# A decode-and-prefill step on one core: V sums moved behind the logits, the pooling mixers into free PSUM banks, the token-row turns spread, heads later, 12 w_out tiles among the cache pages

## The reference

```python
h = rmsnorm(x, norm1_g)
q, k, v, u = split(h @ w_in)               # 8 heads of 128; u is 1024 wide
a = attend(q, k, v)                        # prompt: causal with ALiBi; sample: see below
p = pool_mixer(u)                          # windows 2, 4, 8, 16, then a 256x256 product per group
x = x + concat([a, p]) @ w_out             # w_out: 2048 x 2048
h2 = rmsnorm(x, norm2_g)
x = x + (silu(h2 @ w_gate) * (h2 @ w_up)) @ w_down      # 5632 wide
y = rmsnorm(x, norm_f_g)
```

## Time and profile before

| what | value |
|---|---|
| median of 3 runs | 1420.48 us (1417.19 to 1421.45) |
| profiled execution | 1420.67 us, span of the trace 1418.6 us |
| PE busy | 1352.9 us (95%) |
| DVE, ACT, POOL busy | 712.7, 494.0, 105.0 us |
| moved by DMA | 334.13 MB, mean 236 GB/s |
| mean granted TensorE clock | 0.981 of full speed |

### The profile page before, as it was taken

One profiled execution on the slowest core, in us unless ns is written; L12 is line 12 of the kernel. 1 busy time (PEld: TensorE's weight loads), 2 busy tenths in 40 slices (PEclk: granted clock), 3 DMA queues, 4 the chain that ended last, 5 costly groups with the idle time before them and its releaser, 6 DMA issues.

```text
span 1418.6 us, 27166 instructions
## 1 busy us (share of the span) xinstructions
PE 1352.9 (95%) x10651; PEld 1256.1 (89%) x10651; DVE 712.7 (50%) x1102; ACT 494.0 (35%) x653; POOL 105.0 (7%) x172
## 2 busy tenths in 40 slices
PE   7999999998688899999999999999999999999998
PEld 6987777774466689999999999999999999999997
DVE  7633432324333437746455555555564646455556
ACT  6322222213221225633333334343333333333334
POOL 5038200001000003100000000000000000000003
PEclk9999999998899999999999999999999999999999
DMA  9779999997989854544444444444444444444442
GB/s 353 298 302 380 412 413 410 410 382 254 405 330 412 341 211 177 193 164 166 169 168 163 163 164 170 168 163 163 164 167 170 164 163 164 166 171 164 163 163 97
DMA packets 91750, 334.13 MB, mean 236 GB/s; under 512 B 10465, under 2 KB 10466, under 8 KB 91426
## 3 DMA queue, kind: packets, MB, share of 16 engines
q1 hardware_dynamic: 91682, 333.22, 63.0%
HBM read 327.77 MB, written 5.40 MB: 235 GB/s over the span
## 4 chain that ended last, share of the span: by engine, by line
PE 85%; DMA 5%; DVE 4%; SPq 3%; issue 2%; ACT 1%; DVEq 0%; ACTq 0%
PE banks L1338 26%; PE banks L1339 26%; PE banks L1340 25%; PE banks L1402 3%; DMA w_raw<-in_weights 3%; PE banks L1418 3%; DVE w_lo L808 1%; SPq L422 1%; DMA vpage<-in_cache_v 1%; SPq L436 1%; ACT w_hi L553 1%; DMA kpage<-in_cache_v 1%; PE banks L1346 1%; PE banks L1488 0%; SPq L426 0%
## 5 line engine op out<-in xcount | busy, mean ns | idle before, releaser
L808 DVE TENSOR_TENSOR w_lo<-w_raw,w_hi 128x1024 fp32r<-128x1024 f32 x360 | 442.7, 1235 | 542.6 <-ACT w_hi L553 541.9
L1338 PE MATMUL banks<-hh,w_hi 128*128 128x288 f32 x2176 | 651.2, 299 | 25.2 <-DVE w_lo L808 19.2
L1339 PE MATMUL banks<-hl,w_hi 128*128 128x288 f32 x2176 | 648.3, 298 | 0.0
L1340 PE MATMUL banks<-hh,w_lo 128*128 128x288 f32 x2176 | 645.6, 297 | 0.0
L553 ACT ACTIVATE w_hi<-w_raw 128x1024 fp32r<-128x1024 f32 x360 | 379.4, 1058 | 695.6 <-PE banks L1340 459.1
L1338 PEld LDWEIGHTS banks<-hh,w_hi 128*128 128x128 f32 x2176 | 414.2, 190 | 51.0 <-issue 40.0
L1339 PEld LDWEIGHTS banks<-hl,w_hi 128*128 128x128 f32 x2176 | 414.4, 190 | 0.1
L1340 PEld LDWEIGHTS banks<-hh,w_lo 128*128 128x128 f32 x2176 | 413.3, 190 | 0.0
L1340 PE MATMUL banks<-ah,w_lo 128*128 128x288 f32 x704 | 207.8, 295 | 0.0
L1339 PE MATMUL banks<-al,w_hi 128*128 128x288 f32 x704 | 207.4, 295 | 0.0
L1338 PE MATMUL banks<-ah,w_hi 128*128 128x288 f32 x704 | 206.6, 293 | 0.5 <-DVE al L1171 0.5
(11 more groups left out here) (163 smaller groups left out, 523.0 us busy)
## 6 DMA issues: line engine op xcount, KB each, us to landing
w_raw<-in_weights SPq DMA_DIRECT2D x360, 512.0 KB, 3.2
kpage<-in_cache_k SPq DMA_DIRECT2D x128, 512.0 KB, 6.9
vpage<-in_cache_v SPq DMA_DIRECT2D x120, 512.0 KB, 7.1
kpage<-in_cache_v SPq DMA_DIRECT2D x8, 512.0 KB, 7.8
out_y_prompt<-yt SPq DMA_DIRECT2D x4, 512.0 KB, 3.5
xT<-in_x SPq DMA_DIRECT2D x3, 576.0 KB, 8.8
out_k_new<-z SPq DMA_DIRECT2D x1, 1152.0 KB, 6.6
out_v_new<-z SPq DMA_DIRECT2D x1, 1152.0 KB, 8.9
```

The lines of the kernel that those rows point to most:

```text
L808: V.tensor_tensor(w_lo[:, s, :], w_raw[:, s, :], w_hi[:, u, :].bitcast(F32), ALU.subtract).then_inc(lo_ready, 1)
L1338: PE.matmul(o, wh, xh[:, c, :], start=start and i == 0, stop=False)
L1339: PE.matmul(o, wh, xl[:, c, :], start=False, stop=False)
L1340: last = PE.matmul(o, wl, xh[:, c, :], start=False, stop=stop and i == len(chunks) - 1)
```

## The change

- In steps behind a block's first, PE does `logits`, then `values`, then the tiles; before it was `logits`, one tile, `values`, the rest. At a block's first step it does two tiles (in the head blocks one), `joint_max`, the rest, then `p_turned`.
- DVE makes the low part of a block's first tile at the end of the step before, ahead of `take_values`; `head_lo` stands before `joint_max`.
- ACT makes the high parts of a step's tiles first in the step, ahead of the heads' copies.
- The mixers move from steps 12 to 18 to steps 10, 11, 14 and 15, into the spare logits bank and bank 7 (`PB`).
- The six row turns, in a row at the end of block 4 before, stand now at step 21 (two) and steps 22, 23, 26, 27 (one each), all copied out by ACT.
- Head h has its logits at step 21 + h; before at 19 + h, with head 0 at the very end of step 19. The clearing of `qza` moves from DVE to POOL.
- Block 4 has 8 tiles instead of 10, and the two kvu tiles that are left stand in step 20. Out tiles among the pages: 12 instead of 10 (2, 5, 5 in blocks 5, 6, 7 against 1, 3, 6). Four instead of six stand behind step 31. SP loads out tile 12 at step 30, 13 at step 31, 14 ahead of V units 30 and 31, and 15 behind them.

```diff
-TILE_COUNT = (3, 2, 2, 2) * 4 + (3, 2, 2, 3) + (0, 0, 1, 0, 1, 1, 1, 0) + (2, 1, 2, 1)
+TILE_COUNT = (3, 2, 2, 2) * 4 + (2, 2, 2, 2) + (2, 0, 1, 1) + (2, 1, 1, 1) + (2, 1, 1, 1)
-HEAD0 = NQUADS * KVU_STEPS
-MIX_BLOCK = 7
+HEAD0 = NQUADS * KVU_STEPS + 1
+MIX_AT = {10: 0, 11: 1, 14: 2, 15: 3}
+ROWS_AT = {22: 1, 23: 3, 26: 4, 27: 5}
...
@@ PE, steps of blocks 0 to 4
                 for j in range(1, NQUADS):
+                    n = NQUADS * i + j
                     logits(i, j)
-                    here = TILES_AT[NQUADS * i + j]
-                    tile(here[0])
                     if i:
                         values(i - 1, j - 1)
-                    tiles(here[1:])
-                if i == KVU_STEPS - 1:
-                    pe.wait_ge(z_ready, 24)
-                    rows_turned(0)
-                    rows_turned(1)
+                    if n in MIX_AT:
+                        mixer(2 * MIX_AT[n])
+                        mixer(2 * MIX_AT[n] + 1)
+                    tiles(TILES_AT[n])
+                if i:
                     values(i - 1, NQUADS - 1)
-                    rows_turned(2)
-                    rows_turned(3)
-                    rows_turned(4)
-                    rows_turned(5)
...
@@ PE, steps of blocks 5 to 7
                     logits(i, j)
-                    if j == 0:
+                    if j:
+                        values(i - 1, j - 1)
+                    else:
                         block_sums(i - 1)
                         combine(i - 2)
-                    if h < H:
+                    if h == 0:
+                        pe.wait_ge(z_ready, 24)
+                        rows_turned(0)
+                        rows_turned(2)
+                    if 0 <= h < H:
                         head_logits(h)
-                    bank1_free(h)
-                    head_turned(h - 1, HB[1])
+                    if h == 0:
+                        pe.wait_ge(tok_act, 2)
+                        own_logits(0)
+                    if 1 <= h <= H:
+                        bank1_free(h)
+                        head_turned(h - 1, HB[1])
                     if j == 0:
+                        tiles(here[:1])
                         joint_max(i - 1)
...
@@ DVE, blocks 5 to 7
                     add_tiles(TILES_AT[n - 1])
-                    lo_tiles(TILES_AT[n])
+                    if h == 0:
+                        take_block(11)
+                        q_spread()
+                    lo_tiles(TILES_AT[n][1 if j == 0 else 0:])
                     if j == 0:
                         select_blocks(i - 1)
+                        if 1 <= h <= H:
+                            head_lo(h - 1)
                         joint_max(i - 1)
...
                         if j == NQUADS - 1:
+                            if i < NB - 1:
+                                lo_tiles(TILES_AT[n + 1][:1])
                             take_values(i - 1)
...
@@ POOL, ahead of the low parts of the pooling mix
+            pool.wait_ge(w_used, T_KVU + KVU_TILES)
+            G.memset(qza[:, :, :], 0.0).then_inc(qza_clear, 1)
...
@@ SP, behind the page steps
-            load_out_pool(range(OUT_TAIL + 3, OUT_TAIL + 4))
+            load_out_pool(range(OUT_TAIL + 2, OUT_TAIL + 3))
             load_v(NQUADS * NB - 2)
             load_v(NQUADS * NB - 1)
-            load_out_pool(range(OUT_TAIL + 4, KC))
+            load_out_pool(range(OUT_TAIL + 3, KC))
```

More of the change, by code:

```diff
@@ L484, in _ @@
                 if n == NQUADS * NB - 2:
-                    load_out_pool(range(OUT_TAIL, OUT_TAIL + 2))
+                    load_out_pool(range(OUT_TAIL, OUT_TAIL + 1))
                 if i and j == NQUADS - 1:
@@ L959, in q_spread @@
                 dve.wait_ge(w_used, T_KVU + KVU_TILES)
-                own.link(V.memset(qza[:, :, :], 0.0))
+                dve.wait_ge(qza_clear, 1)
                 V.tensor_copy(qza[:, :, :].rearrange("p b (h s) -> p b h s", s=36)[:, :, :, 0:NQ],
@@ L1445, in rows_turned @@
             def rows_turned(n):
-                if n >= 2:
-                    pe.wait_ge((tok_act, tok_dve)[n % 2], n // 2)
+                if n not in (0, 2):
+                    i = min(u for u in ROWS_AT if ROWS_AT[u] == n) // NQUADS
+                    pe.wait_ge(pt_ready, i)
+                    pe.wait_ge(comb_saved, i - 1)
+                    if n in (3, 5):
+                        pe.wait_ge(tok_act, n if n == 3 else 5)
                 chunk, a, b = tok_src(n)
@@ L1531, in _ @@
                 here = TILES_AT[NQUADS * i]
-                tile(here[0])
+                tiles(here[:2])
                 if i:
                     joint_max(i - 1)
-                tile(here[1])
+                tiles(here[2:])
                 if i:
                     p_turned(i - 1)
-                tiles(here[2:])
                 for j in range(1, NQUADS):
+                    n = NQUADS * i + j
                     logits(i, j)
-                    here = TILES_AT[NQUADS * i + j]
-                    tile(here[0])
@@ L1591, in _ @@
                         own_logits(OWN_AT[h])
+                    if n in ROWS_AT:
+                        rows_turned(ROWS_AT[n])
                     if j == 0:
+                        tiles(here[1:])
                         p_turned(i - 1)
-                    tiles(TILES_AT[n])
+                    else:
+                        tiles(here)
                     if j == NQUADS - 1:
                         values(i - 1, j)
-            i = NB - 1
-            for j in range(NQUADS):
-                here = TILES_AT[NQUADS * i + j]
-                logits(i, j)
-                if j == 0:
-                    block_sums(i - 1)
-                    combine(i - 2)
-                    tile(here[0])
-                    joint_max(i - 1)
-                    tiles(here[1:])
-                    p_turned(i - 1)
-                else:
-                    tile(here[0])
-                    values(i - 1, j - 1)
-                    tiles(here[1:])
-            values(i - 1, NQUADS - 1)
             k0 = OUT_TAIL
```

198 lines of the change are left out of this document (87 added, 111 removed).

## The result

| | before | changed |
|---|---|---|
| median | 1420.97 us (4 runs) | 1395.84 us (4 runs, 1393.75 to 1397.16) |
| profiled execution | 1420.67 us, span 1418.6 | 1393.75 us, span 1391.9 |
| mean granted TensorE clock | 0.981 | 0.993 |

The ratio is 0.9827, 95% interval 0.9811 to 0.9843: 25 us faster, where 1398 was forecast.

The account below looks back on a forecast made before the run. Holes in the page transfers from 300 us to the last V unit were taken as the bound: -30.2 (floor) + 4.0 (holes left) + 3.4 (tail) = -22.8 against 1420.67, so 1397.9, given as 1398; range 1390 to 1412 us.

Parts of the forecast that it names:

- The holes that remain: Transfer holes left from 300 us to the last V unit after the change, taken as 4 us.
- Third hole: Transfer gap at 462 to 473 us, V buffer freed late behind a tile; 5.4 us, counted as gone.
- Second hole: Transfer gap at 385 to 399 us, PE waiting 6.14 us for `dm`; to go, up to 1 us a block staying.
- First hole: Transfer gap at 320 to 360 us, K unit waiting for step 20's logits; 14.2 us, gone but for about 1 us.
- Clearing on POOL: Clearing `qza` on POOL instead of DVE: taken as 4 us long, costing PE 0 to 2 us, counted 0.
- The new wait for ACT: PE waiting for ACT's two copies ahead of `head_values`: some 0.9 us in six steps, 5 us.
- PE's balance: PE's work in the head blocks, 147 to 165 us plus 5, against the floor's 168.4 us: fits, barely.
- The tail: Last V sums behind the last exponentials: PE idles 5 to 8 us, two sums run slower, +3.4 us (0 to 8).
- A: Rival: half to two thirds of PE's idle and half-clock excess stays in the head blocks; 1403 to 1412 us, chance 0.24.
- B: Rival: head-block stream is full at a lower rate, say 358 GB/s, so holes are worth 20.9 us; 1408.7 us, chance 0.03.
- C: Rival: holes move, K loads waiting on SP behind V loads and tiles; within 4 us of 1420.7, chance 0.06.
- D: Rival: slower, PE waiting at `head_values` in eight head steps for ACT, held by late tiles; 1429 us, chance 0.09.

Follow-up runs that it names:

- a_turns_block: The changed kernel with all six row turns in step 21, ahead of head 0; 1394.69 us, ratio 0.9824 to the kernel before.
- a_heads_20: The changed kernel with two row turns, head 0 and own logits in step 20, later heads one step sooner, last two kvu tiles in step 19; 1396.07 us.
- b_v_early: The kernel before with only the V sum moved directly behind the logits in steps behind a block's first; 1416.74 us, ratio 0.9981.
- a_v_late: The changed kernel with the V sums back behind the step's first tile, in head steps behind the head's turn; 1403.87 us, ratio 0.9896 to the kernel before.
- b_lo_early: The kernel before with high parts first on ACT and the low part of a block's first tile a step earlier on DVE (blocks 5 to 7); 1414.19 us.
- b_turns_behind: The kernel before with the six row turns, head 0's logits and first own logits behind the logits of step 20; 1421.89 us, ratio 1.0015.
- a_clear_dve: The changed kernel with `qza` cleared on DVE again instead of POOL; 1397.55 us, ratio 0.9839 to the kernel before.
- b_three: b_turns_behind, b_v_early and b_lo_early together on the kernel before; 1411.85 us, ratio 0.9951.
- a_pe_light: The changed kernel without the high-weight by low-activation product in 28 kvu and 12 out tiles, 42 us less PE work; 1397.52 us, ratio 0.9846 to the kernel before.

## Why the prediction was right, and where not

- *Transfers bound it; the end moves as the last V sum does.* Shown: the table's loss and span go together, the span less that sum's start is the same to 3.2 us in fourteen kernels, the light kernel gains nothing, and 700 us on is unchanged. The forecast landing was 471.4 + 4.0 = 475.4; it was 474.4. The last few us are not the stream's alone: in the changed kernel the landing and PE's list behind the exponentials end together, and in a_turns_block and a_heads_20 that list ends 2 to 3.5 us behind the landing.
- *The holes that remain.* 4.0 forecast, 3.3 measured. The size is right and the place is not: they lie at 440 to 460, around the issue of V units 28 and 29, which is the third hole that I counted as gone, and none is left of the first, nor in the blocks' first steps.
- *Third hole.* That the V sum's place makes it is shown by b_v_early, which closed it, and by a_v_late, where it grew from 3.3 to 9 us. In the changed kernel it shrank from 6.1 us (384 and 190 GB/s) to 3.3. The V sum's place is not the only lever: in b_lo_early, which leaves it alone, the stretches from 460 to 480 moved 285 and 380 GB/s, 3.9 us lost.
- *Second hole.* Shown by b_lo_early: the wait for `dm` fell from 6.14 to 1.8 us; in the changed kernel it is 0.2.
- *First hole.* It went, as forecast, but the cause that I gave is not what the runs show. "Only the logits of step 20 were late" is wrong: b_turns_behind made them early, and the hole moved to the logits of step 21. Nor does the change need its single parts: not the spread turns, not the clearing on POOL, not the step (a_turns_block, a_clear_dve and a_heads_20 each undo one of these and have no hole there). In b_turns_behind and b_three the six turns, head 0's logits, the wait for `qza` (3.62 us) and head 0's own turn and values all stand in step 20, ahead of the logits of step 21; in a_heads_20 only two turns and the logits do, `qza` is ready, and the head's turn comes behind the logits of step 21. So it seems to be the sum of what stands between two K frees. The head's own turn and values are not the main part of it: the kernel before has them in step 20 too, and its logits of step 21 follow those of step 20 after 7.1 us, against 19.9 in b_turns_behind, where the moved work takes 10.3 us. Six turns alone, in a step that is not a block's first (a_turns_block), make no hole; two turns, head 0 and the own logits in a block's first step (a_heads_20) make none either. That it takes both together, the wait for `qza` included, is argued from the timelines; no run has all of it in step 20 of the changed kernel, and it stays open. The new distribution of tiles and the mixers' new places were not tried alone either. That this hole's 14.2 us came out as forecast is therefore in part luck.
- *Clearing on POOL*: I took 4 us, it took 2.02 us. DVE's filling waited 1.2 us for it and PE not at all. On DVE again it costs nothing that can be measured (0.9839 against 0.9827, intervals of 0.003).
- *The new wait for ACT*: 0.9 us six times forecast, 0.7 measured (3.6 + 0.7 = 4.3 us in all), off the bound, since these waits stand in a_pe_light unchanged while PE has time to spare.
- *PE's balance*: "it fits, barely" was too cautious. PE was busy 149.2 of 172.2 us, and 11.3 us of the rest are waits for pages.
- *The tail* is the term of the sum that was mis-sized. I counted +3.4 us for two V sums at the half clock; in the profiled execution they ran at the full one, 3.69 us for both, while the tile ahead of them ran at 0.66 (460 to 465 us) and hid it in the wait for `ss`. The idling of 5 to 8 us did come: from 440 to 467.2 us PE was busy 19.2 of 27.2 us. With 0.7 us fewer lost to holes this is about the 3.9 us between the sum's 1397.9 - 2.1 - 1418.6 = -22.8 and the measured -26.7. But it was no phantom: in the profiled executions of a_turns_block and a_heads_20 the two took 6.05 and 6.17 us, and both spans are 3.4 us longer (1395.3), about 2.4 of them from these sums. The median of the changed kernel is 2.1 us above its profiled execution; that its other executions differ in this way is likely, not shown. That the forecast of 1398 lies only 2.2 us above the median is in part chance.
- *The rivals.* A's remaining PE waits are there in part, but up to the last unit not on the bound. B, the lower rate: the Trainium skill (DMA: Bandwidth & Descriptors, "Where 436 GB/s comes from") has HBM to SBUF at about 358 GB/s per core; the trace disagrees, with 413 GB/s over the 100 us from 200 on and 402 in the head blocks. The same page, under its measured bandwidths, calls 358 each core's part when both cores of a memory domain stream; this program runs on one core, so that case is not tested here. The sum for B (1408.7) also leaves out the 2.2 us between landing and sum that the floor takes off; with them it is 1406.5, which is still far from 1395.8. C, that the holes move, happened to b_turns_behind, but not for C's reason: the K unit waited for PE's work, not for SP's order. D did not: no wait of PE between 300 and 500 us is longer than 3.1 us.

## What to carry to other kernels

Where a stretch of a program hangs on one stream of transfers, add up the time in which the stream was not full: here that sum went with the span to about 6 us over fourteen kernels, while 42 us less work on PE gave nothing. A hole belongs to all the work and waiting between two frees of a buffer pair, so moving that work behind one free hands the hole to the next. Judge the order by when each buffer comes free on the issuing queue, and the last units by what stands between their landing and the end, and by the list that has to be done ahead of the last sum.

## What the runs showed of the hardware

- The page stream (512 KB transfers) held 413 GB/s for 100 us, and 402 over the 172 us of the head blocks, its last hole included.
- POOL cleared 128 x 2304 floats in 2017 ns, DVE in 1978 ns. The Trainium skill (GPSIMD Engine Reference, section 3.1) gives about 1.8 cycles an element as the best case of an unrolled loop, an estimate of 3.5 us, and the trace is faster. The same section has 1.03 cycles for loop bodies of up to two operations, an estimate of 2.0 us, and the trace agrees with that.
- Less work can cost clock: with 139 matmuls fewer in the same 100 us (200 to 300) the granted clock fell from 1.00 to 0.88, and the busy time fell by 8.7 us instead of 18.3. In the head blocks it fell from 0.96 to 0.91.
- The same 64 matmuls of two V sums ran at either level from one kernel to the next: 3.69 us at a clock of 1.00 behind a wait of 0.54 us, and 6.05 us at 0.60 behind a wait of 2.73 us. In the first case the tile ahead of them ran at 0.66, in the second at 1.00, so the stretch of lower clock only stood in another place.
